# A hybrid decoder block: a reordered opening, whole compression runs, and a diagonal solve in two parts

## The chip, the cores and the metric

The kernel runs on one core of a Trainium2 chip. The metric is the device time of one execution in microseconds (us), and what is compared is the median of several executions. The engines are TensorE (PE in the profile, with its weight loads as PEld), VectorE (DVE), ScalarE (ACT), GpSimd (POOL) and SyncE (SP, which here only issues loads).

## The reference

One layer over 256 tokens of width 1024, float32. Everything below is computed; sizes are those of the run.

```
h = RMSNorm(x)                       # x: 256 x 1024
P = h @ W_in                         # q,k,v,z and a,b of 8 DeltaNet heads; q, 3 x (k,v), gates of NSA
yA = GatedDeltaNet(P_A)              # causal conv of 4 taps, L2 norm, chunked delta rule with a
                                     # unit-triangular solve, gated RMSNorm
yB = NSA(P_B)                        # compressed blocks: silu(blocks @ cmp_w1) @ cmp_w2 for k and v,
                                     # plus selected blocks, plus sliding window
x += (sigmoid(gA) * (yA @ W_pa) + sigmoid(gB) * (yB @ W_pb)) @ W_out
x += (silu(h2 @ W_gate) * (h2 @ W_up)) @ W_down          # h2 = RMSNorm(x)
```

## The kernel before, in words

**Chunks.** The weights come as 87 chunks of 1 MB in the fixed order of the list CHUNKS: gk, gq, gv (four each), kc, vc, then nq mixed with cmpk, then ks, kw, cmpv, vs, vw and gz mixed, the gate and projection chunks mga, pa, mgb, pb, four wo, and at last pairs of gu (w_gate and w_up beside each other) with a dn (w_down) after every pair from the second on. A slot n is what the engines do around chunk n. The kernel writes the order of every engine out by hand; nothing is scheduled at run time.

**Splitting.** A float32 product is made as three products of a rounded high part and a rest: hi by hi, hi by lo, lo by hi. SP loads a chunk into one of three buffers `raw` (a fourth, `raw_ahead`, for nq 0 and nq 2); ACT copies it to `w_hi` (L618), DVE subtracts to `w_lo` (L945), each into one of two buffers, and PE then runs the chunk in two halves (`half_chunk`) of 24 matmuls (L1418 to L1420; in gu L1516 and L1519). Chunk n+1 is split while PE runs chunk n. `load_chunk(n)` waits until the chunk before in the same buffer is split. The chunks cmpk and cmpv (four each) are not split: eight small matmuls (L1493) read `raw` directly, four in each half, with a stage of the delta rule between the halves where slot_stages says so.

**Opening.** SP loads x in one transfer, then ident, then chunk 0 in two halves, and after it has waited for the vectors (vec_in, which ACT queued) chunk 1. PE first runs 32 matmuls on ones (`keep_busy`, L1436), transposes two sets of vectors (L1423), runs 5 more, transposes the normalized x in 16 pieces (`to_channels`), and begins chunk 0. Each engine takes one of the two row blocks of x for the sum of squares (ACT L624, DVE L979); DVE makes rstd from both sums in ten small steps; each engine then scales one block. ACT rounds both halves of chunk 0, then evacuates eight tiles of h (`h_hi`, L635); DVE makes the rest of the first half of chunk 0 (L989) and eight tiles of `h_lo` (L971), POOL makes the second (L525). Chunk 0's first half needs for each row tile k the tiles h_hi and h_lo of that k; its second half repeats all k for the other 128 columns. Between the halves PE makes a bias vector from `relb` and `onehot` (L1761, in ps[6]).

**Diagonal solve.** DVE inverts the 16 x 16 diagonal blocks of the delta rule in `solve_diagonal`, once, in the slot of nq 2 (slot 19) after `split_lo(20)`. POOL then stores the result and loads it back in 16 small transfers, and the stage X4 in slot 24 (cmpv 0) waits for them.

**The feed-forward part.** In the slot after a gu chunk its two sums are evacuated: ACT copies one part (gside, uside), DVE adds the other, multiplies with rstd and frees the banks (usum_done), ACT makes the silu, DVE the product (gu_done), and `evacuate_late` splits the product for dn. In the slots gu 1 and gu 2 this comes after the split of the next chunk, in all others before it. In the slot of gu 0 DVE first makes h_lo of the last two row tiles (`h_low`), then splits gu 1.

Of the kernel before, what the change touches and what calls it, by code (L numbers as in the profile page):

```python
# [145 lines left out]
TAIL = range(AT["gz", 2], AT["pa", 3])  # L146

# [10 lines left out]
def slot_solves(n, half):  # L158
    return (n, half) == (AT["nq", 2], 0)
# [28 lines left out]
def hybrid_block(nc, x, norm1_w, w_in, conv_w, a_log, dt_bias, gdn_norm_w, cmp_pe, cmp_w1, cmp_w2,  # L188
# [5 lines left out]
    with ctx:  # L194
# [124 lines left out]
        stream_ps = ps[0:2]  # L319
        gdn_ps = ps[2:5]  # L320
# [7 lines left out]
        first_hi, first_lo, second_lo = sem("first_hi"), sem("first_lo"), sem("second_lo")  # L328
        raw_first = sem("raw_first")
# [3 lines left out]
        x_in, vec_in, ident_in, const_in, levels_in, small_in, misc_in = sem("x_in"), sem("vec_in"), sem("ident_in"), sem("const_in"), sem("levels_in"), sem("small_in"), sem("misc_in")  # L333
# [136 lines left out]
        def _(sp):  # L470
            sp.dma_start(x_sb[:], x[0].rearrange("(t p) d -> p t d", p=P)).then_inc(x_in, 16)
# [124 lines left out]
        def _(act):  # L596
# [26 lines left out]
            act.wait_ge(x_in, 16)  # L623
            nc.scalar.activation(xn_sb[:, 0, :], x_sb[:, 0, :], ACT.Square, accum_out=scol["x"][:, 0:1]).then_inc(xss, 1)  # L624
            act.wait_ge(rstd_ready, 1)
            nc.scalar.activation(xn_sb[:, 1, :], x_sb[:, 1, :], ACT.Copy, scale=scol["x"][:, 5:6]).then_inc(xn_done, 1)
            act.wait_ge(raw_first, 16)
            nc.scalar.activation(w_hi[0][:, 0:KT // 2, :], raw[0][:, 0:KT // 2, :], ACT.Copy).then_inc(first_hi, 1)
            act.wait_ge(raw_in[0], 16)
# [30 lines left out]
            def evacuate(n):  # L660
                kind, i = CHUNKS[n]
                if kind == "gu":
# [5 lines left out]
                    if i == 0:  # L668
                        act.wait_ge(rows_mm, 1)
                        nc.scalar.activation(rstd_rows[:], ps[6][:, 0:SEQ], ACT.Copy).then_inc(rows_out, 1)  # L670
                    act.wait_ge(gsum_done, i + 1)
# [10 lines left out]
                if kind in ("gk", "gq", "gv"):  # L682
# [3 lines left out]
                    else:  # L686
                        act.wait_ge(pre_dve, 3)
                    nc.scalar.activation(cin[k % 2][:, :, CONV - 1:CONV - 1 + SEQ], bank, ACT.Copy)
                    for a in range(2):
                        ins = nc.scalar.activation(cacc[k % 2][:, a, :], bank[:, a, :], ACT.Copy, scale=tap(k, a, CONV - 1))  # L690
# [167 lines left out]
            for n in range(len(CHUNKS) + 1):  # L858
                kind, i = CHUNKS[n] if n < len(CHUNKS) else (None, 0)
                first_half_out = n < len(CHUNKS) and is_wide(n) and i % 2  # L860
                if n == 0:
                    split_hi(1)
                else:
                    conv_phase = n <= FIRST_STAGE_SLOT
                    if not conv_phase and n not in (AT["gu", 1], AT["gu", 2]):
                        evacuate(n - 1)
# [5 lines left out]
                    if conv_phase or n in (AT["gu", 1], AT["gu", 2]):  # L872
                        evacuate(n - 1)
                    if CHUNKS[n - 1] not in LAST_OF_KIND:
# [55 lines left out]
        def _(dve):  # L930
# [37 lines left out]
            def h_low(before, row, tiles=range(KT)):  # L968
                for k in tiles:
# [8 lines left out]
            dve.wait_ge(x_in, 16)  # L978
            nc.vector.tensor_tensor_reduce(xn_sb[:, 1, :], x_sb[:, 1, :], x_sb[:, 1, :], 1.0, 0.0, ALU.mult, ALU.add,  # L979
                                           accum_out=scol["x"][:, 1:2]).then_inc(xss, 1)  # L980
            dve.wait_ge(xss, TT)
            link(radicand(scol["x"][:, 2:4], scol["x"][:, 0:2], 1.0 / D_MODEL, EPS))
            rsqrt(scol["x"][:, 4:6], scol["x"][:, 2:4], scol["x"][:, 6:8], rstd_ready)
            dve.wait_ge(rstd_ready, 1)
            nc.vector.tensor_scalar(xn_sb[:, 0, :], x_sb[:, 0, :], scol["x"][:, 4:5], None, ALU.mult).then_inc(xn_done, 1)
            dve.wait_ge(pre_pe, 2)
# [6 lines left out]
            link(nc.vector.tensor_copy(cols_a[:], ps[7][:, 0:CONV * 24]))  # L993
            link(nc.vector.tensor_scalar(wk[:], cols_b[:, ROW_KN:ROW_KN + 3], cols_b[:, ROW_QN:ROW_QN + 1], DH ** -0.5, ALU.mult, ALU.mult))
            link(nc.vector.tensor_scalar(zw[:], cols_b[:, ROW_GDN:ROW_GDN + 1], 0.5, None, ALU.mult))
            dve.wait_ge(pre_pe, 3)
            nc.vector.tensor_copy(bias_v[:], ps[6][0:HEADS, 0:384]).then_inc(pre_dve, 1)
# [112 lines left out]
            def solve_diagonal():  # L1110
# [4 lines left out]
                dve.wait_ge(sub_in, 16)  # L1115
                link(nc.vector.memset(sub_t[:], 0.0))
                link(nc.vector.memset(view(sub_t, 0, (down, SUB)), 1.0))
                four = (4 * down, 4)
                link(nc.vector.tensor_copy(view(sub_t, SUB, four), view(sub_m, 1, four)))
                for r in (2, 3):  # L1120
# [3 lines left out]
                for n in (4, 8):  # L1124
# [17 lines left out]
                dve.wait_ge(solved, 1)  # L1142
                nc.vector.tensor_copy(view(sub_tt, 0, (SUB, SUB), (1, SUB)), view(sub_t, 0, (1, SUB), (SUB, SUB))).then_inc(solved, 1)
# [90 lines left out]
            def evacuate(n):  # L1234
                kind, i = CHUNKS[n]
                if kind == "gu":
# [7 lines left out]
                    if i > 0:  # L1244
                        dve.wait_ge(uside, i + 1)
                        nc.vector.tensor_tensor(usum[i % 2][:], usum[i % 2][:], gu_banks(i)[1][:, 0:SEQ], ALU.add).then_inc(usum_done, 1)
                    dve.wait_ge(usum_done, i + 1)
# [59 lines left out]
            for n in range(len(CHUNKS) + 1):  # L1307
                kind, _ = CHUNKS[n] if n < len(CHUNKS) else (None, 0)
                if n == 0:
                    split_lo(1)  # L1310
                else:
                    if n > FIRST_STAGE_SLOT and n not in (AT["gu", 1], AT["gu", 2]):
                        evacuate(n - 1)
# [531 lines left out]
```

## Time and profile before

| what | value |
|---|---|
| median of 3 runs | 580.57 us (580.56 to 581.29) |
| profiled execution, its own time | 580.86 us |
| its span (first to last instruction) | 579.0 us |
| PE busy | 566.9 us, 98% of the span |
| DVE busy | 387.7 us, 67% |
| ACT busy | 299.2 us, 52% |
| POOL busy | 66.5 us, 11% |
| DMA | 98.23 MB, mean 170 GB/s |
| chain that ended last, by engine | PE 88%, DVE 7%, issue 2%, ACT 2% |

PE is busy nearly all the time, so a change can gain in two ways: by taking instructions or their overhead off PE, or by closing the places where PE stands idle before an instruction. In a row of the timeline, the bracket at the end is that idle time with what ended it. "issue" means that nothing in the profile's records explains it.

### The profile page before, as it was taken

The page shows a single profiled execution, that of the slowest core. Times are in us where ns is not written, and L with a number is a line of the kernel's source. Part 1 is how long each engine was busy: PE and PEld are TensorE (multiplying, and loading weights), DVE is VectorE, ACT ScalarE, POOL GpSimd, SP SyncE. Part 2 cuts the span into 40 slices and gives each one's busy share as a digit, 9 for nine tenths or more (in the row PEclk, how much of TensorE's full clock was granted, in tenths as well). Part 3 has the DMA queues.
Part 4 walks back from the last instruction along what each step waited for, and adds up shares of the span by engine and source line. Part 5 has one row for each costly group of instructions (what it writes and reads, how often), then busy time and mean ns, then how long its engine had stood idle before and what let it go on. Part 6 is the DMA issues. An engine that isn't in the chain of part 4 may idle for free.

```text
span 579.0 us, 9820 instructions
## 1 busy us (share of the span) xinstructions
PE 566.9 (98%) x3914; PEld 499.6 (86%) x3914; DVE 387.7 (67%) x624; ACT 299.2 (52%) x470; POOL 66.5 (11%) x81
## 2 busy tenths in 40 slices
PE   9999999999999999989999999999999999999997
PEld 8999999899788888778888888898788888888886
DVE  4778898855766652897865574757756566566664
ACT  5569555515435556637463634366454544545542
POOL 4011210761600000090000000000000000000000
PEclk9999999999999999999999999999999999999999
DMA  7954477595755425423533445575466756667631
GB/s 242 268 180 142 151 192 241 103 294 181 209 148 167 140 79 190 146 77 142 161 132 122 149 168 207 157 198 164 146 192 175 214 180 184 186 179 218 167 124 72
DMA packets 99382, 98.23 MB, mean 170 GB/s; under 512 B 4818, under 2 KB 83719, under 8 KB 99338
## 3 DMA queue, kind: packets, MB, share of 16 engines
q1 hardware_dynamic: 97024, 93.69, 52.6%
q0 software_dynamic: 1808, 2.78, 2.6%
q10 hardware_dynamic: 506, 1.14, 0.6%
q8 instruction: 31, 0.51, 0.4%
q14 instruction: 13, 0.11, 0.1%
HBM read 96.46 MB, written 1.84 MB: 170 GB/s over the span
## 4 chain that ended last, share of the span: by engine, by line
PE 88%; DVE 7%; issue 2%; ACT 2%; POOL 0%; DVEq 0%; ACTq 0%; POOLq 0%
PE ps L1418 18%; PE ps L1420 17%; PE ps L1419 17%; PE ps L1516 13%; PE ps L1519 6%; PE ps L1423 4%; PE ps L1596 4%; DVE w_lo L945 2%; PE ps L1436 2%; PE ps L1751 2%; PE ps L1493 2%; PE ps L1725 1%; PE ps L1627 1%; ACT w_hi L618 1%; DVE cacc L1040 1%
## 5 line engine op out<-in xcount | busy, mean ns | idle before, releaser
L945 DVE TENSOR_TENSOR w_lo<-raw,w_hi 128x2048 fp32r<-128x2048 f32 x76 | 175.2, 2305 | 96.0 <-ACT w_hi L618 95.9
L618 ACT ACTIVATE w_hi<-raw 128x2048 fp32r<-128x2048 f32 x76 | 145.3, 1912 | 81.2 <-PE ps L1420 75.4
L1516 PE MATMUL ps<-h_both,w_hi 128*128 128x512 f32 x352 | 122.8, 397 | 1.0 <-DVE w_lo L945 0.6
L1519 PE MATMUL ps<-h_both,w_lo 128*128 128x256 f32 x352 | 91.1, 279 | 0.0
L1418 PE MATMUL ps<-h_both,w_hi 128*128 128x256 f32 x288 | 82.8, 288 | 0.5 <-DVE h_both L971 0.3
L1419 PE MATMUL ps<-h_both,w_hi 128*128 128x256 f32 x288 | 81.4, 283 | 0.0
L1420 PE MATMUL ps<-h_both,w_lo 128*128 128x256 f32 x288 | 81.4, 283 | 0.0
L1516 PEld LDWEIGHTS ps<-h_both,w_hi 128*128 128x128 f32 x352 | 63.9, 188 | 15.1 <-issue 2.8
L1519 PEld LDWEIGHTS ps<-h_both,w_lo 128*128 128x128 f32 x352 | 66.4, 189 | 3.3
L1418 PE MATMUL ps<-w_hi,h_both 128*128 128x512 f32 (+1 forms) x160 | 58.1, 363 | 4.5 <-DVE zs L1274 2.9
L1418 PEld LDWEIGHTS ps<-h_both,w_hi 128*128 128x128 f32 x288 | 55.1, 191 | 3.8 <-issue 3.6
L1420 PE MATMUL ps<-w_hi,h_both 128*128 128x512 f32 (+1 forms) x160 | 55.6, 348 | 0.0
L1419 PE MATMUL ps<-w_lo,h_both 128*128 128x512 f32 (+1 forms) x160 | 55.5, 347 | 0.0
L1419 PEld LDWEIGHTS ps<-h_both,w_hi 128*128 128x128 f32 x288 | 55.2, 192 | 0.0
L1420 PEld LDWEIGHTS ps<-h_both,w_lo 128*128 128x128 f32 x288 | 55.2, 192 | 0.0
L1418 PEld LDWEIGHTS ps<-w_hi,h_both 128*128 128x128 f32 x160 | 30.2, 189 | 11.6 <-issue 6.0
L1418 PE MATMUL ps<-w_hi,g_hi 128*128 128x512 f32 x88 | 34.4, 391 | 1.1 <-issue 1.1
L1040 DVE SCALAR_TENSOR_TENSOR cacc<-cin,cols_a,cacc 128x256 f32<-128x256 f32 x72 | 35.0, 553 | 0.1
L1420 PE MATMUL ps<-w_hi,g_lo 128*128 128x512 f32 x88 | 34.3, 389 | 0.0
L1419 PE MATMUL ps<-w_lo,g_hi 128*128 128x512 f32 x88 | 34.3, 389 | 0.0
L1420 PEld LDWEIGHTS ps<-w_hi,h_both 128*128 128x128 f32 x160 | 30.2, 189 | 4.0
L1419 PEld LDWEIGHTS ps<-w_lo,h_both 128*128 128x128 f32 x160 | 30.3, 189 | 3.2
(361 smaller groups left out, 938.5 us busy)
## 6 DMA issues: line engine op xcount, KB each, us to landing
raw<-in_w_in SPq DMA_DIRECT2D x31, 1024.0 KB, 5.2
raw<-in_w_gate SPq DMA_DIRECT2D x22, 512.0 KB, 3.9
raw<-in_w_up SPq DMA_DIRECT2D x22, 512.0 KB, 5.2
raw<-in_w_down SPq DMA_DIRECT2D x11, 1024.0 KB, 4.9
raw<-in_cmp_w SPq DMA_DIRECT2D x8, 1024.0 KB, 6.5
raw<-in_w_proj_a SPq DMA_DIRECT2D x4, 1024.0 KB, 5.7
raw<-in_w_proj_b SPq DMA_DIRECT2D x4, 1024.0 KB, 5.1
raw<-in_w_out SPq DMA_DIRECT2D x4, 1024.0 KB, 5.1
```

Of the source, the lines that this page charges most:

```text
L618: nc.scalar.activation(w_hi[s % NSPL][:], raw[RAW_OF[n]][:], ACT.Copy).then_inc(hi_done, 1)
L945: nc.vector.tensor_tensor(w_lo[s % NSPL][:], raw[RAW_OF[n]][:], w_hi[s % NSPL][:].bitcast(f32), ALU.subtract).then_inc(lo_done, 1)
L1040: ins = nc.vector.scalar_tensor_tensor(acc, src[:, a, j:j + SEQ], tap(k, a, j), acc, ALU.mult, ALU.add)
L1418: pe.matmul(bank, lhs(lh), rhs(rh), start=start, stop=False)
L1419: pe.matmul(bank, lhs(lh), rhs(rl), start=False, stop=False)
L1420: return pe.matmul(bank, lhs(ll), rhs(rh), start=False, stop=stop)
L1423: return pe.transpose(o, i, ident[0:n, 0:n])
L1436: pe.matmul(ps[1][:, 0:P], ones_sq[:], ones_sq[:], start=True, stop=True)
L1493: last = pe.matmul(ps[6][g:g + 32, 0:CW], flat[:, i * KT + j, :], raw[RAW_OF[n]][:, j, :], start=(i == 0 and j < 4), stop=(i == 3 and j >= 4))
L1516: cross = lambda stop: pe.matmul(banks[part][:], hi[:, k, part * P:(part + 1) * P], h_both[:, :, k, :], start=(k == 0), stop=stop)
L1519: end = pe.matmul(banks[part][:, 0:SEQ], lo[:, k, part * P:(part + 1) * P], h_hi[:, k, :], start=False, stop=False)
L1596: mm = lambda q, lhsT, rhs, start=True, stop=True: pe.matmul(b4[:, q, :], lhsT, rhs, start=start, stop=stop)
```

## The change

Five things, all on one core and with the same arithmetic:

1. x is loaded in two transfers, one for each row block. DVE sums block 0 and half of block 1, ACT the other half of block 1; one more small DVE step adds the two. Scaling is divided the same way. `keep_busy` runs 20 and 3 times in place of 32 and 5, and the bias matmul moves ahead of the second of them, into ps[1].
2. Chunk 0 runs both column halves for each row tile k (banks ps[0] and ps[6]), hi by hi first, so that only the last pair of each k needs h_lo. ACT rounds the second half of chunk 0 between h_hi tiles 3 and 4. Chunk 1 is split in two halves of rows with semaphores of their own. The copies of conv taps (cols_a) and two small DVE steps move behind that split.
3. The eight compression matmuls of a chunk run in one go, in half 1 for cmpk 0 and in half 0 for all others.
4. `solve_diagonal` runs in two parts: up to blocks of 8 in slot 17 (nq 1, half 1), the rest in slot 19 as before.
5. In the slots gu 2, gu 3 and dn 0 the evacuation is divided: the part that frees the banks ("a") runs before the split of the next chunk, silu and product ("b") after it. In the slot gu 0 `h_low` runs after the split of gu 1.

```diff
+GU_OPENING = (AT["gu", 2], AT["gu", 3], AT["dn", 0])
+def cmp_half(n):
+    return 1 if CHUNKS[n] == ("cmpk", 0) else 0
-def slot_solves(n, half):
-    return (n, half) == (AT["nq", 2], 0)
+SOLVES = {(AT["nq", 1], 1): 0, (AT["nq", 2], 0): 1}
...
-            sp.dma_start(x_sb[:], x[0].rearrange("(t p) d -> p t d", p=P)).then_inc(x_in, 16)
+            for t in range(TT):
+                sp.dma_start(x_sb[:, t, :], x[0, t * P:(t + 1) * P, :]).then_inc(x_tile[t], 16)
... ACT, opening
-            nc.scalar.activation(xn_sb[:, 0, :], x_sb[:, 0, :], ACT.Square, accum_out=scol["x"][:, 0:1]).then_inc(xss, 1)
+            nc.scalar.activation(xn_sb[:, 1, 512:], x_sb[:, 1, 512:], ACT.Square, accum_out=scol["c"][:, 2:3]).then_inc(xss, 1)
...
-            nc.scalar.activation(w_hi[0][:, KT // 2:, :], raw[0][:, KT // 2:, :], ACT.Copy).then_inc(hi_done, 1)
             for k in range(KT):
+                if k == 4:
+                    act.wait_ge(raw_in[0], 16)
+                    nc.scalar.activation(w_hi[0][:, KT // 2:, :], raw[0][:, KT // 2:, :], ACT.Copy).then_inc(hi_done, 1)
... ACT and DVE, slot 0: chunk 1 in two halves
+                    for k, done in ((slice(0, KT // 2), early_hi), (slice(KT // 2, KT), hi_done)):
+                        nc.scalar.activation(w_hi[1][:, k, :], raw[1][:, k, :], ACT.Copy).then_inc(done, 1)
...
             h_low(0, ROW_N1)
+            dve.wait_ge(pre_pe, 3)
+            nc.vector.tensor_copy(bias_v[:], ps[1][0:HEADS, 0:384]).then_inc(pre_dve, 1)
+            for k, split, done in ((slice(0, KT // 2), early_hi, early_lo), (slice(KT // 2, KT), None, lo_done)):
+                nc.vector.tensor_tensor(w_lo[1][:, k, :], raw[1][:, k, :], w_hi[1][:, k, :].bitcast(f32), ALU.subtract).then_inc(done, 1)
+            nc.vector.tensor_copy(cols_a[:], ps[7][:, 0:CONV * 24]).then_inc(cols_set, 1)
... ACT and DVE, every slot n
+                    if not conv_phase and n != AT["gu", 1]:
+                        evacuate(n - 1, "a" if n in GU_OPENING else "ab")
...
+                    elif n in GU_OPENING:
+                        evacuate(n - 1, "b")
... PE, opening
-            keep_busy(32)
+            keep_busy(20)
...
-            keep_busy(5)
-            pe.wait_ge(xn_done, TT)
+            pe.wait_ge(misc_in, 80)
+            pe.matmul(ps[1][0:HEADS, 0:384], relb[:], onehot[:], start=True, stop=True).then_inc(pre_pe, 1)
+            keep_busy(3)
+            pe.wait_ge(xn_done, TT + 1)
... PE, compression chunks
-                    for j in range(half * KT // 2, (half + 1) * KT // 2):
+                    for j in range(KT):
... PE, chunk 0
+                        for k in range(KT):
+                            pe.wait_ge(first_hi if k < KT // 2 else hi_done, 1)
+                            pe.wait_ge(h_hi_done, k + 1)
+                            for o, c in both:
+                                pe.matmul(o, hi[:, k, c], h_hi[:, k, :], start=(k == 0), stop=False)
+                            if k < KT // 2:
+                                pe.wait_ge(first_lo, 1)
+                                for o, c in both:
+                                    pe.matmul(o, lo[:, k, c], h_hi[:, k, :], start=False, stop=False)
+                            pe.wait_ge(h_lo_done, k + 1)
+                            for o, c in both:
+                                pe.matmul(o, hi[:, k, c], h_lo[:, k, :], start=False, stop=False)
+                        pe.wait_ge(second_lo, 1)
+                        for o, c in both:
+                            for k in range(KT // 2, KT):
+                                last = pe.matmul(o, lo[:, k, c], h_hi[:, k, :], start=False, stop=(k == KT - 1))
```

## Rows read from the trace of the kernel before

**Rows 1.** Windows: busy us and instructions by engine, granted clock, DMA share, GB/s.
```profile
229.00:251.00 22.00, 18.91 (x103) 14.84 (x102) 18.82 (x36) 11.28 (x25) 3.72 (x2) 1.00 0.30 100
```

**Rows 2.** Timeline of PE, opening: start us, us, engine, line, what [idle before].
```profile
1.03 9.80 PE L1436 MATMUL ps<-ones_sq 128*128 128x128 f32 x64 [1.03 <-POOL ones_sq L511]
...
11.98 1.91 PE L1423 MATMUL ps<-ident,xn_sb 128*128 128x128 f32 x16
...
14.22 0.36 PE L1418 MATMUL ps<-h_both,w_hi 128*128 128x256 f32 x1 [0.33 <-DVE h_both L971]
...
17.49 0.81 PE L1761 MATMUL ps<-onehot,relb 33*8 33x384 f32 x2
...
21.29 0.36 PE L1418 MATMUL ps<-h_both,w_hi 128*128 128x256 f32 x1
```

**Rows 3.** The same timeline, the other engines of the opening.
```profile
6.04 1.23 DVE L979 CUSTOM_DVE_ANT_0 xn_sb<-x_sb 128x1024 f32<-128x1024 f32 x1 [5.13 <-DMA x_sb<-in_x]
...
9.29 0.75 DVE L985 TENSOR_SCALAR xn_sb<-x_sb,s_x 128x1024 f32<-128x1024 f32 x1
9.59 0.37 SPq L487 DMA_DIRECT2D raw<-in_w_in  x1
...
12.42 2.45 POOL L525 TENSOR_TENSOR w_lo<-raw,w_hi 128x1024 fp32r<-128x1024 f32 x1 [7.12 <-ACT w_hi L630]
...
12.62 3.03 ACT L635 ACTIVATE h_both<-ps,cols_b 128x256 fp32r<-128x256 f32 x8 [0.29 <-PE ps L1423]
13.59 3.23 DVE L971 SCALAR_TENSOR_TENSOR h_both<-ps,cols_b,h_both 128x256 fp32r<-128x256 f32 x8 [0.95 <-ACT h_both L635]
```

**Rows 4.** Timeline of POOL, the last load that the bias matmul waits for.
```profile
3.80 0.54 POOL L521 DMA_DIRECT2D par<-in_dt_bias  x1
```

**Rows 5.** DMA issues: what, queue, count, KB each, us to landing.
```profile
par<-in_dt_bias POOLq DMA_DIRECT2D x1, 4.0 KB, 5.7
```

**Rows 6.** Groups of PE instructions from 3 to 6 us: busy us, mean ns.
```profile
L1436 PE MATMUL ps<-ones_sq 128*128 128x128 f32 x16 | 3.6, 418 | 0.0
```

**Rows 7.** The chain that ended last: start us, us, what (an fp32 matmul counts twice).
```profile
119.20 1.00 PE ps L1493 x16
...
130.08 0.12 PE ps L1418
...
165.54 0.57 PE ps L1493 x8
```

**Rows 8.** Timeline of DVE, slots 19 to 22.
```profile
138.68 2.29 DVE L945 TENSOR_TENSOR w_lo<-raw,w_hi 128x2048 fp32r<-128x2048 f32 x1 [3.46 <-ACT w_hi L618]
140.97 0.27 DVE L1116 MEMSET sub_t<- 128x256 f32 x1
...
144.26 1.08 DVE L1132 TENSOR_TENSOR sub_x<-sub_m,sub_t 128x512 f32<-128x512 f32 x1
...
148.19 2.29 DVE L945 TENSOR_TENSOR w_lo<-raw,w_hi 128x2048 fp32r<-128x2048 f32 x1
```

**Rows 9.** Timeline of PE where chunk 22 (ks) begins.
```profile
150.58 0.36 PE L1418 MATMUL ps<-w_hi,h_both 128*128 128x256 f32 x1 [1.40 <-issue]
```

**Rows 10.** Timeline of PE, starts of gu 1, gu 3 and dn 0.
```profile
395.17 0.47 PE L1516 MATMUL ps<-h_both,w_hi 128*128 128x512 f32 x1 [0.65 <-DVE w_lo L945]
...
407.30 0.48 PE L1516 MATMUL ps<-h_both,w_hi 128*128 128x512 f32 x1 [0.24 <-DVE usum L1246]
...
414.26 0.47 PE L1418 MATMUL ps<-w_hi,g_hi 128*128 128x512 f32 x1 [1.11 <-issue]
```

**Rows 11.** Timeline of DVE, h_low in slot gu 0, split of dn 0.
```profile
391.95 0.88 DVE L971 SCALAR_TENSOR_TENSOR h_both<-ps,cols_b,h_both 128x256 fp32r<-128x256 f32 x2 [2.73 <-ACT h_both L855]
...
411.87 2.29 DVE L945 TENSOR_TENSOR w_lo<-raw,w_hi 128x2048 fp32r<-128x2048 f32 x1 [1.39 <-ACT w_hi L618]
```

**Rows 12.** Timeline of ACT, split of gu 1 and of gu 3.
```profile
388.61 1.92 ACT L618 ACTIVATE w_hi<-raw 128x2048 fp32r<-128x2048 f32 x1 [1.33 <-PE ps L1420]
...
401.74 1.90 ACT L618 ACTIVATE w_hi<-raw 128x2048 fp32r<-128x2048 f32 x1
```

More of the change, by code:

```diff
@@ L670, in evacuate @@
                         nc.scalar.activation(rstd_rows[:], ps[6][:, 0:SEQ], ACT.Copy).then_inc(rows_out, 1)
+                if kind == "gu" and "b" in steps:
                     act.wait_ge(gsum_done, i + 1)
@@ L1123, in solve_diagonal @@
                     link(nc.vector.tensor_reduce(view(sub_t, r * SUB, four, (1, r)), view(sub_x, 0, (r * r, 4), (r, r), (1, r)), AX.X, ALU.add))
-                for n in (4, 8):
+                for n in (4, 8)[part:part + 1]:
                     firsts = range(0, SUB, 2 * n)
@@ L1232, in unit, with evacuate @@
                                             ALU.mult).then_inc(p_done, 1)
-            def evacuate(n):
+            def evacuate(n, steps="ab"):
                 kind, i = CHUNKS[n]
-                if kind == "gu":
+                if kind == "gu" and "a" in steps:
                     dve.wait_ge(gside, i + 1)
@@ L1246, in evacuate @@
                         nc.vector.tensor_tensor(usum[i % 2][:], usum[i % 2][:], gu_banks(i)[1][:, 0:SEQ], ALU.add).then_inc(usum_done, 1)
+                if kind == "gu" and "b" in steps:
                     dve.wait_ge(usum_done, i + 1)
@@ L1308, in _ @@
                 kind, _ = CHUNKS[n] if n < len(CHUNKS) else (None, 0)
[L1309 to L1313, printed above, removed]
+                if n > 0:
+                    if n > FIRST_STAGE_SLOT and n != AT["gu", 1]:
+                        evacuate(n - 1, "a" if n in GU_OPENING else "ab")
                     if CHUNKS[n - 1] in LAST_OF_KIND:
                         evacuate_late(n - 1)
-                    if n == AT["gu", 0]:
-                        h_low(KT, ROW_N2, (KT - 2, KT - 1))
                     if n == AT["ks", 0] + 1:
@@ L1435, in keep_busy @@
                 for _ in range(times):
[L1436 removed]
+                    pe.matmul(ps[0][:, 0:P], ones_sq[:], ones_sq[:], start=True, stop=True)
             pe.wait_ge(ones_set, 2)
[L1439 removed]
+            keep_busy(20)
             pe.wait_ge(ident_in, 16)
@@ L1469, in half_chunk @@
                     hi, lo = w_hi[s % NSPL], w_lo[s % NSPL]
-                    if half == 0 and n > 0:
+                    if half == 0 and n > 1:
                         pe.wait_ge(hi_done, s + 1)
@@ L1473, in half_chunk @@
                         wait_bank(pe, n)
-                elif half == 0:
+                elif half != cmp_half(n):
+                    return None
+                else:
                     pe.wait_ge(raw_in[RAW_OF[n]], 16 * loads_before(n))
@@ L1484, in half_chunk @@
                     c = 0 if kind == "cmpk" else 1
-                    if i == 0 and half == 0:
+                    if i == 0:
                         pe.wait_ge(flat_done, 4 * (c + 1))
@@ new lines, in half_chunk @@
+                    if n == 1 and half == 0:
+                        for k in range(KT):
+                            if k == 0:
+                                pe.wait_ge(pre_dve, 3)
+                                pe.wait_ge(early_hi, 1)
+                                pe.wait_ge(early_lo, 1)
+                            if k == KT // 2:
+                                pe.wait_ge(hi_done, 2)
+                                wait_lo(pe, 1)
+                            last = three(((hi, lo), acts), bank, lambda a: a[:, k, 0:P], lambda a: a[:, k, :], k == 0, k == KT - 1)
+                        return last
@@ L1757, in _ @@
                     last = half_chunk(n, half)
-                    last.then_inc(half_done, 1)
-                    if n == 0 and half == 0:
-                        pe.wait_ge(misc_in, 80)
-                        pe.matmul(ps[6][0:HEADS, 0:384], relb[:], onehot[:], start=True, stop=True).then_inc(pre_pe, 1)
+                    if last is not None:
+                        last.then_inc(half_done, 1)
                     if n == 3 and half == 0:
```

95 lines of the change are left out of this document (55 added, 40 removed).

## The prediction

> **What bounds the kernel now.** I read the shares of busy time first: PE is busy 98% of the span, and 88% of the chain that ended last is PE's. So what counts is PE's own work and the few places where it stands idle. I then read the timeline of PE for idle brackets and went to each that the change touches: before the first matmul on h [rows 2], before chunk 22 [rows 9], and before gu 1, gu 3 and dn 0 [rows 10]. Two further stalls lie between 229 and 251 us, where PE is busy 18.91 of 22.00 us [rows 1]; nothing in the diff touches what they wait for. Last I read the other engines around each place [rows 3, 8, 11, 12] to see what is late next. Everywhere else PE runs without a gap, so a microsecond won at one place reaches the end, as long as the engine that feeds PE there is itself paced by PE.
>
> **Opening.** Before, PE runs 64 matmul records on ones until 10.83 us (1.03 + 9.80), two small transposes, five more calls on ones, and transposes x from 11.98 to 13.89 [rows 2]. But rstd is ready at 9.29 and x is scaled soon after (9.29 + 0.75 on DVE) [rows 3]: PE's own filler makes it late. Now the filler is 24 records shorter. At the pace of the transposes, 1.91 / 16 = 0.12 us each [rows 2], it ends at 10.83 - 24 x 0.12 = 7.95 us. PE then waits for the vectors. SP, which waits for the same ones before it issues chunk 1, issues at 9.59 [rows 3], so they are there just before. The last load for the bias matmul is issued at 3.80 and takes 5.7 us [rows 4, 5], so 9.5: no later. From 9.6 come two small transposes (2 x 0.12), the bias matmul (0.74: its 0.81 less the overlap of two records) and three calls on ones (6 x 0.12): 9.6 + 0.24 + 0.74 + 0.72 = 11.3. Scaled x must be there by then. DVE now sums one and a half blocks: if both halves of x land together at 6.0, that is 1.23 + 0.62, and one step of 0.2 more; rstd comes 0.8 later, at 10.1, and scaling ends at 10.1 + 0.75 + 0.4 = 11.25. If block 0 lands over a microsecond earlier, DVE has it summed by 6.0, and rstd is at about 9.1 and scaling ends at 10.3. Either way 11.3 holds. Transposes of x end at 11.3 + 1.9 = 13.2.
>
> Chunk 0 before takes from 14.22 to 21.29, 7.07 us [rows 2]. Of that 0.74 is the bias matmul. Its 48 matmuls at the steady 0.12 us [rows 7] are 5.76; the other 0.6 is the first half paced by DVE's h_lo, 3.23 / 8 = 0.40 us a tile [rows 3] against 0.36 for three matmuls, and a short gap before chunk 1. With both column halves per tile PE needs 0.72 us a tile in the first four and 0.48 in the last four, both above 0.40. It can also start on hi by h_hi before any h_lo exists. So chunk 0 runs from 13.2 to 19.0, and chunk 1 starts 21.29 - 19.0 = 2.3 us earlier.
>
> What is late next? ACT: h_hi 0 to 3 from 0.64 after the transposes start (as 12.62 is to 11.98), 0.38 a tile, so 11.9 to 13.5; the second half of w_hi, about 1.0, to 14.5; h_hi 4 to 7 to 16.0. PE asks for h_hi 4 at 13.2 + 4 x 0.72 = 16.1. POOL's 2.45 us [rows 3] then ends at 17.0; PE asks for it at 18.0. DVE ends h_lo at 16.9, then the bias copy (some 0.5) and chunk 1's two halves, 1.2 each (half of 2.29 [rows 8] and a little), at 18.6 and 19.8. PE asks at 19.0 and at 19.0 + 12 x 0.12 = 20.4. The margins are 0.4 and 0.6 us, thin but there. Because ACT takes two more small instructions in the evacuation of chunk 0, nothing but DVE's conv 0 waits longer. I take 2.2 us. Lower bound: if the conv slots are paced by DVE and not by PE, only what DVE is ahead counts. Its split of chunk 1 ended at 21.1 before and its three moved small steps now end at 20.4: 0.7 us. Upper bound: the 2.3 us.
>
> The rows also show a state of the clock: from 3 to 6 us a matmul on ones has a mean of 418 ns [rows 6], though the later ones follow each other at 0.12 us, and it was the filler that PE ran in between. Now PE idles from about 7.95 to 9.6. The Trainium skill, "TensorE: Matmul & The Clock Gate", Part 1, says that the throttled state is the default, that activity releases it, and that an idle PE falls back to the lower clock. The trace speaks against it for pauses of this size: with 3.1 us of idle between 229 and 251 the granted clock stays 1.00 [rows 1]. By the row the opening gains 2.2; a fall is a rival below.
>
> **Compression.** Four matmuls in a run take 0.57 us, eight in one run 1.00 [rows 7]: 2 x 0.57 - 1.00 = 0.14 us saved wherever a stage stood between. That is so in cmpk 0 and in the four cmpv. In cmpk 0 the stage now starts 0.57 us earlier, right behind DVE's evacuation of the stage before, so I count nothing there. Four times 0.14 is 0.55 (between 0.4 and 0.7). The stages after a cmpv run get more time for their inputs, and the raw buffer is freed earlier.
>
> **Diagonal solve.** Chunk 22 (ks) waits 1.40 us [rows 9]. Its low part runs on DVE from 148.19 to 150.48, directly behind the solve, which begins at 140.97 [rows 8]. Part 0 is 144.26 - 140.97 = 3.3 us long. In slot 17 it lies in DVE's idle time of 3.46 us before 138.68 [rows 8], just fitting; behind it waits the low part of chunk 20, which PE needs only when it is through with chunk 19. Part 1 then ends 3.3 us earlier, DVE is free at 144.9, and the low part of chunk 22 needs 2.29 after ACT's high part. It suffices that ACT is done by 146.9; DVE found it ready at 148.19. So the whole 1.40 goes. If the high part came late, or part 0 waited for its input from memory, up to 1.4 would stay. The loads that POOL makes from the result also start 3.2 us earlier, so X4 waits for nothing.
>
> **Feed-forward.** In slot gu 0 ACT's high part of gu 1 is done at 390.5 [rows 12], but DVE runs h_low until 392.83 first [rows 11], and gu 1 waits 0.65 [rows 10]. Now the split runs from 390.6 to 392.9, and h_low's first tile ends at 393.3. PE asks for it at about 393.0. So 0.65 goes and about 0.35 comes: 0.3 gained. In the slots gu 2 and gu 3, part "a" ahead of the split frees the banks at once: the 0.24 on usum before gu 3 [rows 10] goes. For dn 0, PE waited 1.11 [rows 10] until the low part ended at 411.87 + 2.29 = 414.16 [rows 11]; DVE itself waited for ACT, which was behind with silu and product of gu 1 and the copies of gu 2. In the new order ACT has in slot gu 3 only two copies (0.7 together) between the end of gu 2 and its high part, and DVE finds it after part "a". I get 409.4 for the high and 411.7 for the low part, on the old scale, against PE's 412.5 on the same scale. The 1.11 goes. In slot gu 2 the copies put ACT's high part of gu 3, at 401.74 before [rows 12], 0.3 later, its low part to 406.3, and PE needs it at 406.7. Together 0.3 + 0.24 + 1.11 = 1.65; if only one of the two thin margins fails, 0.5 less.
>
> **Sum.** 2.2 + 0.55 + 1.40 + 1.65 = 5.8 us. The profiled execution took 580.86 us, which gives 575.1; the median of the runs is 0.29 lower, so 574.8.
>
> **Rivals.** (a) As worked out: 574.8, own range 573.9 to 575.7. Chance 0.62. (b) DVE, not PE, carries the lateness of the opening. For: in the conv slots DVE has 2.29 + 3.2 of every 5.76 us. Against: PE shows no gap there that DVE ends. The opening gives 0.7, in all 4.3: 576.3. Chance 0.14. (c) One of the stalls at ks or dn 0 only changes its cause: 1.1 to 1.4 less, 576.1. For: the fit of 3.3 in 3.46 and two margins under half a microsecond; against: PE needs those parts later than they come. Chance 0.11. (d) The clock falls in the pause after the filler. PE's work from 9.6 on then takes twice as long; for 3 us of it that is 3 us, the opening ends 0.8 later than before, and the total is 2.8 faster: 577.8. By the skill's page this would be the outcome if the pause counted as idle enough; the filler of the kernel before is what speaks for it, the unbroken 1.00 in the row [rows 1] speaks against it. Chance 0.07. (e) Slower: the third load into the first raw buffer waits for POOL's half of chunk 0, which now ends at 17.0 and not 14.87. If the loads then set the pace, each slot takes 1.05 MB at the mean 170 GB/s, 6.2 us in place of 5.76, 0.4 more a slot. It decides from 17 such slots on (7.0 us). Against it: the load is needed at 24.7, 7.7 us after its issue. 582, chance 0.02. (f) The change does not do what it says, because each gain ends in a wait of the next fixed chain, such as those between 229 and 251: 580.5. Against: these chains start from PE. Chance 0.04.
>
> **Range and chances.** From 573.8 to 577.0 hold (a), (b) and (c), some 0.85 with the tails cut. About 0.2%, 1.2 us, is what a measurement can tell from no change. Faster by more: (a) to (d) and a part of (f), 0.95; within it 0.03; slower 0.02.
>
> **What would show it.** Chunk 1's first matmul at 19.1 (late by DVE: a bracket on w_lo before it); the records on ones at 0.12 apart after the pause, else the clock; runs of 1.00 in all eight compression chunks; no bracket before ks; brackets of at most 0.35 in gu 0 and none before gu 3 and dn 0. A new bracket in slots 2 to 12, or a stall that reappears at ks, would make the number wrong.

## The result, and the profile after

The changed kernel takes 575.39 us (median of 4 runs, 574.49 to 576.73) against 580.88 us for the kernel before (4 runs, 580.56 to 581.29). The ratio of the times is 0.991, with a 95% interval of 0.9894 to 0.9923: faster by 5.5 us. The forecast was 574.8 us, in the range 573.8 to 577.0. The profiled execution took 575.23 us, its span is 573.2 us, 5.8 less than before.

The first lines of the page of the changed kernel. PE is still the bound, and busy 4.5 us less; 3.1 of that is filler (46 records on ones in place of 74).

```profile
span 573.2 us, 9771 instructions
## 1 busy us (share of the span) xinstructions
PE 562.4 (98%) x3886; PEld 496.5 (87%) x3886; DVE 390.3 (68%) x629; ACT 298.4 (52%) x472; POOL 66.3 (12%) x81
```

PE's timeline of the opening answers to [rows 2]. Columns as there.

```profile
1.03 7.04 PE L1470 MATMUL ps<-ones_sq 128*128 128x128 f32 x40 [1.03 <-POOL ones_sq L520]
9.71 0.27 PE L1457 MATMUL ps<-ident,rows_a 96*128 96x96 f32 x1 [1.64 <-DMA rows_b<-in_cmp_pe]
...
11.50 1.91 PE L1457 MATMUL ps<-ident,xn_sb 128*128 128x128 f32 x16
13.17 0.48 PE L1596 MATMUL ps<-h_both,w_hi 128*128 128x256 f32 x2
...
19.02 0.28 PE L1452 MATMUL ps<-h_both,w_hi 128*128 128x256 f32 x1
```

Filler until 8.07, a pause of 1.64 us for the vectors, then no gap: chunk 1 starts at 19.02 and not at 21.29. Block 0 of x lands early enough for DVE to start its sum at 4.80, which is the second of the two cases forecast. Behind PE, the engines of [rows 3] finish in time: DVE scaled x by 10.16 (9.68 + 0.48), POOL has the second low part at 17.16, and DVE ends chunk 1's two halves at 19.80. (The lines are from DVE's and POOL's timeline.)

```profile
9.68 0.48 DVE L1010 TENSOR_SCALAR xn_sb<-x_sb,s_x 128x512 f32<-128x512 f32 x1
...
17.46 2.34 DVE L1025 TENSOR_TENSOR w_lo<-raw,w_hi 128x1024 fp32r<-128x1024 f32 x2
```
```profile
14.74 2.42 POOL L534 TENSOR_TENSOR w_lo<-raw,w_hi 128x1024 fp32r<-128x1024 f32 x1 [9.46 <-ACT w_hi L641]
```

The list of PE's waits (total, times, longest) holds all that is left. ("issue" is a wait that nothing in the records explains.) The 1.40 before ks [rows 9] is gone: its first matmul starts at 146.93 with no bracket, 3.65 earlier. The 0.65, 0.24 and 1.11 of [rows 10] are gone too, but 0.54 us stand before gu 3.

```profile
PE ps L1452 <- DVE zs L1308: 3.0, 2, 1.6
PE ps L1457 <- DMA rows_b<-in_cmp_pe: 1.6, 1, 1.6
PE ps L1470 <- POOL ones_sq L520: 1.0, 1, 1.0
PE ps L1457 <- DVE AXb L1102: 0.6, 1, 0.6
PE ps L1556 <- issue: 0.5, 1, 0.5
PE ps L1559 <- DVE h_both L991: 0.3, 1, 0.3
PE ps L1452 <- issue: 0.2, 1, 0.2
```

How far PE is ahead of the kernel before, by the same matmul in both timelines (some of the rows first, those of the changed kernel, then two of the kernel before):

```profile
104.62 0.66 PE L1457 MATMUL ps<-ident,kT 128*128 128x128 f32 x4 [0.58 <-DVE AXb L1102]
...
146.93 0.39 PE L1452 MATMUL ps<-w_hi,h_both 128*128 128x256 f32 x1
...
239.26 0.47 PE L1452 MATMUL ps<-w_hi,h_both 128*128 128x512 f32 x1 [1.40 <-DVE zs L1308]
...
403.07 0.47 PE L1556 MATMUL ps<-h_both,w_hi 128*128 128x512 f32 x1 [0.54 <-issue]
```
```profile
106.95 0.66 PE L1423 MATMUL ps<-ident,kT 128*128 128x128 f32 x4 [0.58 <-DVE AXb L1071]
...
243.45 0.47 PE L1418 MATMUL ps<-w_hi,h_both 128*128 128x512 f32 x1 [1.40 <-DVE zs L1274]
```

| place | before | after | earlier by |
|---|---|---|---|
| chunk 1 | 21.29 | 19.02 | 2.27 |
| the wait on AXb (0.58 in both) | 106.95 | 104.62 | 2.33 |
| first matmul after the stage in cmpk 0 | 115.36 | 113.19 | 2.17 |
| ks | 150.58 | 146.93 | 3.65 |
| first wait on zs (1.40 in both) | 243.45 | 239.26 | 4.19 |
| gu 3 | 407.30 | 403.07 | 4.23 |
| dn 0 | 414.26 | 408.75 | 5.51 |
| last matmul | 575.31 | 569.55 | 5.76 |

### The profile page after: what moved, and what is told of

Same layout as the page of the kernel before. It is cut to its first block, busy times and chain, and to the rows that moved or that the text cites. A ratio compares the mean times of both kernels' runs of the same rounds, so it can differ in the third digit from the quotient of the medians.

```text
span 573.2 us, 9771 instructions
## 1 busy us (share of the span) xinstructions
PE 562.4 (98%) x3886; PEld 496.5 (87%) x3886; DVE 390.3 (68%) x629; ACT 298.4 (52%) x472; POOL 66.3 (12%) x81
## 4 chain that ended last, share of the span: by engine, by line
PE 89%; DVE 6%; ACT 2%; issue 1%; DMA 1%; ACTq 0%; DVEq 0%
PE ps L1452 17%; PE ps L1454 17%; PE ps L1453 17%; PE ps L1556 14%; PE ps L1559 7%; PE ps L1457 4%; PE ps L1660 4%; DVE w_lo L965 2%; PE ps L1815 2%; PE ps L1531 1%; PE ps L1789 1%; DMA rows_b<-in_cmp_pe 1%; PE ps L1691 1%; ACT w_hi L627 1%; DVE cacc L1071 1%
## 5 line engine op out<-in xcount | busy, mean ns | idle before, releaser
L965 DVE TENSOR_TENSOR w_lo<-raw,w_hi 128x2048 fp32r<-128x2048 f32 x75 | 172.9, 2306 | 95.2 <-ACT w_hi L627 95.1
L627 ACT ACTIVATE w_hi<-raw 128x2048 fp32r<-128x2048 f32 x75 | 143.3, 1911 | 78.5 <-PE ps L1454 68.9
L1559 PE MATMUL ps<-h_both,w_lo 128*128 128x256 f32 x352 | 91.3, 280 | 0.3 <-DVE h_both L991 0.3
L1452 PE MATMUL ps<-h_both,w_hi 128*128 128x256 f32 x272 | 77.8, 286 | 0.2 <-issue 0.2
L1453 PE MATMUL ps<-h_both,w_hi 128*128 128x256 f32 x272 | 76.9, 283 | 0.0
L1454 PE MATMUL ps<-h_both,w_lo 128*128 128x256 f32 x272 | 76.9, 283 | 0.0
L1556 PEld LDWEIGHTS ps<-h_both,w_hi 128*128 128x128 f32 x352 | 63.9, 188 | 14.2 <-issue 2.0
L1559 PEld LDWEIGHTS ps<-h_both,w_lo 128*128 128x128 f32 x352 | 66.4, 189 | 4.0 <-issue 0.6
L1452 PEld LDWEIGHTS ps<-h_both,w_hi 128*128 128x128 f32 x272 | 52.1, 192 | 2.5 <-issue 2.5
L1453 PEld LDWEIGHTS ps<-h_both,w_hi 128*128 128x128 f32 x272 | 52.1, 192 | 0.0
L1454 PEld LDWEIGHTS ps<-h_both,w_lo 128*128 128x128 f32 x272 | 52.1, 192 | 0.0
```

Source lines behind the costliest of these rows:

```text
L627: nc.scalar.activation(w_hi[s % NSPL][:], raw[RAW_OF[n]][:], ACT.Copy).then_inc(hi_done, 1)
L965: nc.vector.tensor_tensor(w_lo[s % NSPL][:], raw[RAW_OF[n]][:], w_hi[s % NSPL][:].bitcast(f32), ALU.subtract).then_inc(lo_done, 1)
L1452: pe.matmul(bank, lhs(lh), rhs(rh), start=start, stop=False)
L1453: pe.matmul(bank, lhs(lh), rhs(rl), start=False, stop=False)
L1454: return pe.matmul(bank, lhs(ll), rhs(rh), start=False, stop=stop)
L1556: cross = lambda stop: pe.matmul(banks[part][:], hi[:, k, part * P:(part + 1) * P], h_both[:, :, k, :], start=(k == 0), stop=stop)
```

## The experiments

The kernel before took 580.77 us (18 runs) beside the first four kernels, 580.58 (13 runs) beside the next four, and 580.48 (9 runs) beside the last four.

**The opening alone, and the rest without it.** The first kernel takes from the change only the opening (points 1 and 2); the second only points 3 to 5.

```diff
 open_only: changed kernel, with
-SOLVES = {(AT["nq", 1], 1): 0, (AT["nq", 2], 0): 1}
+SOLVES = {(AT["nq", 2], 0): (0, 1)}
-                    for j in range(KT):
+                    for j in range(half * KT // 2, (half + 1) * KT // 2):
... and evacuation and h_low in the order of before
 rest_only: kernel before, with cmp_half, SOLVES and GU_OPENING of the changed kernel
```

> The opening alone (x in two loads, both halves of chunk 0 per row tile, chunk 1 split in halves, shorter filler); compression, solve and feed-forward as before. If the five parts add up and PE paces the conv slots: chunk 1 begins at 19.0 us as in the changed kernel, and the whole is 2.3 us faster than before (578.6 on a median of 580.9). Rival: the opening's gain reaches the end only together with the others, because DVE or the solve's loads hold their own times; then under 1 us is left, and idle brackets grow at ks or X4.

> Everything but the opening. If the parts add up: 5.6 less 2.3, so 3.3 us faster than before (577.6). If the parts lean on each other (the solve's part 0 fits only because of the opening, or the other way round), it is 2.3 or less, and a bracket stands before ks.

The opening alone: 578.85 us (9 runs, 578.32 to 580.42), 1.9 less; ratio 0.9973 [0.9963, 0.9983]. The rest alone: 577.23 us (4 runs), 3.5 less; 0.9938 [0.9923, 0.9953]. Together 5.46, and the whole change gave 5.49. So the opening's lead is not eaten on the way. In the profile of open_only PE is 3.0 ahead at the AXb wait (this execution's vectors came early, at 8.74), and it keeps that until gu 1. That speaks against DVE pacing the conv slots.

The second kernel showed a wait that the prediction had excluded: the stage X4 on POOL's small loads (PE's timeline).

```profile
165.54 2.08 PE L1646 MATMUL ps<-Db,ATb 64*64 64x64 f32 x64 [0.25 <-DMA DTb<-sub_dt]
```

**The solve alone, the feed-forward part alone.** Kernel before with one point of the change each.

```diff
 solve_only
-    return (n, half) == (AT["nq", 2], 0)
+SOLVES = {(AT["nq", 1], 1): 0, (AT["nq", 2], 0): 1}
 gu_only
+GU_OPENING = (AT["gu", 2], AT["gu", 3], AT["dn", 0])
... evacuate(n - 1, "a" / "b") and h_low as in the change
```

> The diagonal solve in two parts alone. Theory: the bracket of 1.40 us before ks goes and nothing else changes, 1.4 us faster (579.5). Rival: part 0 in slot 17 is held up by GpSimd's clearing of Db, as the 1.49 us copy of the changed kernel suggests, so far that chunk 20 is late; then a new bracket before nq 3 and less than 1 us gained.

> The feed-forward opening alone (evacuation in two parts, h_low behind the split of gu 1). Theory from the trace of the changed kernel: gu 1 0.3 us earlier, gu 3 no earlier than that less its new wait of about 0.5, dn 0 about 1.3 earlier, and 0.2 to 0.3 more behind it: 1.5 us faster (579.4). Rival: the wait before dn 0 went only because the kernel was 4 us ahead of its loads; then it stands here again, and under 0.5 us is gained.

Solve: 579.36 us (10 runs), 1.4 less, 0.9977 [0.9968, 0.9987], and no bracket before ks. Feed-forward: 578.48 us (4 runs), 2.3 less, 0.9961 [0.9946, 0.9975]. The last matmul of the second is 2.41 earlier, but 0.35 of that is there already in the opening, which this kernel doesn't change (first matmul on h at 13.86, not 14.22: the 64 filler records end at 10.18 here and at 10.83 there). That leaves 2.1, more than in the whole change (1.57). rest_only, which also has the old opening, gains 2.0 there. Part of the difference stands before gu 3: a wait of 0.19 in both, 0.54 in the changed kernel.

**The pause of PE in the opening.** The first filler is cut to 2 calls, so that PE idles 6.9 us.

```diff
-            keep_busy(20)
+            keep_busy(2)
```

> The changed kernel with 2 calls on ones in place of the first 20, so PE stands idle from about 2 us until the vectors land (8.7 to 9.7 us in the traces so far). Theory of the clock: the pause is now long, PE comes out of it at the lower of its two levels, the 16 transposes of x take over 3 us and the first matmuls on h follow each other at 0.21 to 0.24 us; chunk 1 begins 2 to 3 us later and the whole is 2 to 3 us slower than the changed kernel. Rival: the filler is of no use, chunk 1 begins at the same time, no difference.

```profile
9.13 0.39 PE L1457 MATMUL ps<-ident,rows_a 96*128 96x96 f32 x1 [6.88 <-DMA rows_b<-in_cmp_pe]
...
12.41 3.43 PE L1457 MATMUL ps<-ident,xn_sb 128*128 128x128 f32 x16
```

578.25 us (10 runs, 576.84 to 580.55), 0.9961 [0.9945, 0.9976], 2.9 more than the changed kernel. The transposes of x take 3.43 us in place of 1.91, chunk 0 runs at full pace from 15.6, and chunk 1 starts at 21.43: 2.41 later, though the vectors came 0.58 earlier, so 3.0 us by the clock. The ten runs lie in two groups of five, 576.84 to 577.65 and 578.84 to 580.55; the profile is of the first (577.61, 2.4 more than the profiled execution of the changed kernel), and what the second group lost on top is not known.

**The compression chunk of the delta stage.** cmpk 0 runs its matmuls in half 0, ahead of the stage between the halves.

```diff
 def cmp_half(n):
-    return 1 if CHUNKS[n] == ("cmpk", 0) else 0
+    return 0
```

> The changed kernel with the whole compression run of cmpk 0 in half 0, ahead of the stage that transposes, and not behind it. Theory: the changed kernel lost 0.16 us there because the 16 transposes start right behind the stage before, wait for its banks and stretch from 2.00 to 2.29 us; with the run of 1.00 us ahead they take 2.00 again and the saving of 0.14 comes: 0.3 us faster than the changed kernel, seen in the trace rather than in the median. Rival: the stretch is due to ACT's copies of the transposes, which then wait still: no difference.

Between the AXb wait and the first matmul behind the stage lie 8.18 us (106.71 to 114.89), against 8.57 in the changed kernel (104.62 to 113.19) and 8.41 before. So this order gains 0.39 there, and keeps it: the zs wait comes 134.24 us after the AXb wait, 134.64 in the changed kernel. Yet the time is 576.72 us (4 runs, 576.45 to 577.01), 0.9929 [0.9914, 0.9944]: 1.3 more than the changed kernel. The opening shows why (PE's timeline, then windows with PEclk, the granted clock, third from the end):

```profile
10.18 0.27 PE L1457 MATMUL ps<-ident,rows_a 96*128 96x96 f32 x1 [2.37 <-DMA rows_b<-in_cmp_pe]
...
11.97 3.40 PE L1457 MATMUL ps<-ident,xn_sb 128*128 128x128 f32 x16
...
21.11 0.28 PE L1452 MATMUL ps<-h_both,w_hi 128*128 128x256 f32 x1
```
```profile
12.00:15.00 3.00, 3.00 (x18) 3.00 (x16) 1.19 (x4) 2.14 (x5) 0.00 (x0) 0.53 1.09 365
15.00:18.00 3.00, 3.00 (x25) 3.00 (x24) 2.22 (x7) 3.00 (x7) 2.42 (x1) 0.90 1.11 337
```

This is what rival (d) describes: the vectors landed late, the pause was 2.37 us, and then, with PE busy again, the clock fell to half for about 3 us. Chunk 1 is 2.09 late: 0.47 by the vectors, 1.38 by the transposes (3.05 us from the first of them to the first matmul on h, in place of 1.67) and 0.25 by the first matmuls on h. So the low clock cost 1.6 us. The edit lies at 112 us, and nothing of it runs in the opening; that all four runs of this kernel had the low clock (0.997) stays unexplained.

**The memset of Db, and gu 0's silu and product.** In the changed kernel DVE's small copy at the head of part 0 takes 1.49 us; before, the same copy took 0.17. POOL's memset runs at the same time.

```profile
133.50 1.49 DVE L1151 COPY sub_t<-sub_m 128x4 f32<-128x4 f32 x1
```
```profile
133.16 1.80 POOL L579 MEMSET Db<- 128x2048 f32 x1 [5.16 <-DVE w_lo L965]
```

One kernel puts the memset behind the stores of the solve, the other gives silu and product of gu 0 to the slot of gu 2.

```diff
 db_late
-            nc.gpsimd.memset(Db[:], 0.0).then_inc(d_init, 1)
             pool.wait_ge(solved, 1)
...
             pool.dma_start(sub_dt, sub_tt[:]).then_inc(sub_back, 16)
+            nc.gpsimd.memset(Db[:], 0.0).then_inc(d_init, 1)
 gu0_late, ACT and DVE
+                    if n == AT["gu", 2]:
+                        evacuate(n - 2, "b")
+                        evacuate_late(n - 2)
-                        evacuate(n - 1)
+                        evacuate(n - 1, "a" if n == AT["gu", 1] else "ab")
```

> The changed kernel with GpSimd's clearing of Db moved from before the solve's result to behind the two stores of it. Theory: the 4-element copy that takes 1.49 us in part 0 of the solve takes so long only because GpSimd clears Db (1.80 us) at the same time; it takes 0.17 again, the low part of chunk 20 starts at about 136.5 instead of 137.6, the result is there 1.1 us earlier, and PE is not faster since it did not wait: no difference in time (within 0.1 us). Rival: the copy waits for its input from memory; then it stays 1.5 us long or gets a bracket.

> The changed kernel with silu, product and high part of gu 0 moved from slot gu 1 to slot gu 2, behind the split of gu 3. Theory: gu 3 waits 0.54 us (0.19 in two other runs) because ACT's split of gu 3 stands behind silu, product and g_hi of gu 0, which wait on rstd and DVE; with them moved the split starts about 1.2 us earlier and the bracket before gu 3 goes: 0.2 to 0.5 us faster. Rival: the wait only moves on to dn 0, whose high and low parts of gu 0 and gu 1 now come later: no gain, a bracket before dn 0.

```profile
133.23 0.17 DVE L1151 COPY sub_t<-sub_m 128x4 f32<-128x4 f32 x1
```

The copy is back at 0.17 and the next split starts 1.1 us earlier behind it; but PE needs 134.63 us from the AXb wait to the zs wait (104.36 to 238.99), against 134.64. The median, 574.83 us (4 runs, 0.9894 [0.9878, 0.9911]), is the changed kernel's. The stretched copy was real and hidden. With gu0_late, 574.77 us (4 runs, 0.9895 [0.988, 0.991]), the bracket before gu 3 is gone, but the wait has moved one chunk on, to dn 0 (PE's timeline):

```profile
408.04 0.47 PE L1458 MATMUL ps<-w_hi,g_hi 128*128 128x512 f32 x1 [0.38 <-issue]
```

**Closing the pause; x in one load; all together.** A repeat of the changed kernel stands beside them.

```diff
 filler_26
-            keep_busy(20)
+            keep_busy(26)
 x_one_load
-            for t in range(TT):
-                sp.dma_start(x_sb[:, t, :], x[0, t * P:(t + 1) * P, :]).then_inc(x_tile[t], 16)
+            sp.dma_start(x_sb[:], x[0].rearrange("(t p) d -> p t d", p=P)).then_inc(x_tile[0], 16)
 best_26: filler_26 with the edits of cmpk0_first, db_late and gu0_late
```

> The changed kernel once more, beside the kernel with the longer filler. Theory (the clock falls in the pause in some executions): most runs at 574.4 to 575.6, some one in four at 576.3 to 577.2 with a mean granted clock of 0.997 or less. Rival (one execution was disturbed by something else): all within 574.3 to 575.8.

> As the changed kernel, but the first filler is 26 calls in place of 20, so that PE idles about 0 to 0.7 us instead of 1.2 to 2.4 us before the vectors come. Theory (the pause lets the clock fall in some executions, and then costs 1.6 to 2 us): no execution shows the fall, transposes of x at 0.12 us each in the profile, the median is 574.5 to 575.0 and all runs lie within 0.6 us of each other. Rival (the spread comes from when the vectors land and not from the clock): median and spread as those of the repeat of the changed kernel, or 0.2 to 0.7 higher, because the longer filler ends behind the vectors in the executions where they land early.

> As the changed kernel, but x comes in one transfer; the division of the sums and of the scaling stays. In the changed kernel DVE had the scale at 9.7 us and PE began the transposes of x only at 11.5, behind the vectors, the bias matmul and the filler. Theory (the two transfers bring nothing): DVE's sum of block 0 begins 1 to 1.5 us later, scaled x is ready at 10.3 to 11.2, the time is as the repeat of the changed kernel within 0.3 us. Rival (DVE's chain is then late, since it sums one and a half blocks): a bracket on the scaled x before its transposes and 0.3 to 1 us more.

> The changed kernel with four edits: cmpk 0 runs in half 0 like the others, the memset of Db comes behind the stores of the solve, silu and product of gu 0 move one slot later, and the first filler is 26 calls. Theory: cmpk 0 gives 0.4, the two others 0.1 to 0.2 each, and the clock never falls: median 573.9 to 574.4, so 0.6 to 1.0 below the changed kernel's. Rival (the gains of the last two are noise and cmpk 0's ends in the next fixed chain): within 0.3 of the kernel that has only the longer filler.

| kernel | median us (runs) | single runs | ratio |
|---|---|---|---|
| changed, again | 575.02 (4) | 574.56, 574.83, 575.22, 576.47 | 0.9908 [0.9895, 0.9922] |
| filler_26 | 575.54 (4) | 574.95, 575.42, 575.66, 575.98 | 0.9912 [0.9899, 0.9926] |
| x_one_load | 575.78 (4) | 575.12, 575.34, 576.22, 576.49 | 0.9917 [0.9904, 0.9931] |
| best_26 | 574.50 (5) | 574.11, 574.16, 574.50, 574.65, 576.18 | 0.9899 [0.9886, 0.9913] |

*The clock.* Of the 8 runs of the changed kernel two have a mean granted clock of 0.997, and they are the 576.73 and the 576.47; the other six are 574.49 to 575.56. With the filler of 20 calls such a clock (0.997 or less) came in 10 of 33 runs, over all kernels with the new opening (4 of the 10 are those of cmpk0_first); with 26 calls in 1 of 9 (the 576.18). That points the way the theory says, but the counts are too small to show that the longer filler cures it. In the profiled executions pauses of 0.17 to 1.64 us went without a fall; those of 2.07 (x_one_load) and 2.37 us were followed by one.

*x.* With one transfer DVE's sum of block 0 starts at 6.01, not 4.80, and scaled x is ready at 11.34 (the prediction had 11.25 for this case). The vectors came at 9.32, and the transposes came 1.07 us after the last filler began, in place of 0.77: 0.3 us of waiting for x. So the second transfer would have been worth 0.3 here, where the vectors were early; with vectors later by that much it would be worth nothing (an argument, not a run). Medians can't tell 575.78 from 575.02, because two of the four runs had the low clock.

*The longer filler didn't pay* in its profiled execution, and the loss is not in the opening. Up to the AXb wait filler_26 is 0.26 ahead of the changed kernel (104.36); at the zs wait it is 0.88 behind (240.14). The stage X4 lies between (timelines of PE, ACT and SP of filler_26):

```profile
164.97 0.68 PE L1691 MATMUL ps<-Db,ATb 64*64 64x64 f32 x16 [0.73 <-ACT AXb L791]
```
```profile
161.38 1.91 ACT L627 ACTIVATE w_hi<-raw 128x2048 fp32r<-128x2048 f32 x1 [5.74 <-DMA raw<-in_w_in]
```
```profile
147.29 1.56 SPq L496 DMA_DIRECT2D raw<-in_w_in  x1
```

and the same two instructions of the changed kernel:

```profile
159.79 1.91 ACT L627 ACTIVATE w_hi<-raw 128x2048 fp32r<-128x2048 f32 x1 [3.93 <-DMA raw<-in_w_in]
```
```profile
147.52 0.53 SPq L496 DMA_DIRECT2D raw<-in_w_in  x1
```

This weight load was under way for 12.3 us in the changed kernel, 14.1 in filler_26 and 13.6 in best_26; before, ACT never waited for it (issued at 150.56, split at 159.42). ACT splits it when it lands, and only then evacuates the tiles that X4 needs. In the changed kernel that split ends at 161.70, 1.2 us before X4 begins; in filler_26 it ends at 163.29, 0.7 us after X4 has begun. In filler_26 X4 with its surroundings takes 6.19 us (162.63 to 168.82) and in best_26 5.68, against 5.08 in the changed kernel. So in the profile of best_26 the 0.39 of cmpk 0 (seen again: 104.13 to 112.31 is 8.18) is lost at X4, and what is left, 0.5 us by medians, is within the intervals. No kernel of these is shown to be faster than the changed one.

The loss does not come from being earlier. In filler_26 the load is issued as long after the AXb wait as in the changed kernel (42.93 us, 42.90); gu0_late, at 104.18 even further ahead, lost nothing (134.64 us to the zs wait); cmpk0_first issued it 0.39 sooner, as best_26 did, had it in 12.2 us and kept its gain. What sets the two profiles apart is SP's issue, 1.56 and 1.36 us long; in the seven other profiles with the whole change it is 0.53 or 0.54, and the load takes 11.6 to 12.5. In both, a load of instructions (queue q8 in the list of DMA queues) falls between 146 and 147 us, beside that issue; in the changed kernel it comes between 152 and 153. A longer filler means more instructions for PE, which could move that load, but that this stretches the issue is not shown, and with one profile of each kernel the two may also be chance.

## Why the prediction was right, step by step

**Opening, 2.2: measured 2.27 at chunk 1 and 2.33 at 106 us.** The times on the way were forecast as 7.95, 9.6, 11.3, 13.2 and 19.0, and came as 8.07, 9.71, 11.50, 13.17 and 19.02. Both h parts were in time and POOL too. "9.5: no later" for the last load of the bias matmul held only because the vectors were late: in open_only, where they came at 8.74, the bias matmul waited another 0.22 us for that load. The single row that the rest hangs on, the time when the vectors land, is the one that varies: 8.74 to 10.18 us in the eight profiles where PE waited for them. My sum took one execution's value for a constant.

**Compression, 0.55: measured 0.38.** Between ks and the zs wait, where the four cmpv lie, 0.54 are gained (3.65 to 4.19): as forecast. In cmpk 0 I had counted nothing; it loses 0.16 (2.33 to 2.17), since with the stage first the transposes of AXb (109.97) come while ACT is still splitting a chunk (until 110.58), and wait for ACT to evacuate them: 16 take 2.29 us in place of 2.00. cmpk0_first shows that the other order would gain.

**Solve, 1.40: measured 1.4 in solve_only,** and 3.65 - 2.17 = 1.48 in the change. Part 0 took 4.6 us and not 3.3, because of the copy; the low part of chunk 20 started 1.1 us later against PE than before, and PE still didn't wait for it. The margin was larger than the 3.46 I compared it with, since what counts is when PE asks. "X4 waits for nothing" was wrong as a rule: it waited 0.25 in rest_only for exactly these loads.

**Feed-forward, 1.65: measured 1.57** (5.76 - 4.19), by two errors that cancel. The step that failed is gu 3: "its low part to 406.3, and PE needs it at 406.7". On that scale, which is the time here plus 4.23, the low part ended at 407.2 (402.97 + 4.23), and 0.54 was waited. The low part was late because ACT's high part was, at 402.89 in place of the forecast 402.0: its two copies cost 0.53 and not 0.3, and the silu of gu 0 in front of them came 0.62 later than before (401.06, 400.44), which the sum had left out. Against it, 0.25 us come after dn 0 has begun, which I hadn't seen: before, dn 0 to gu 4 took 5.78 us, and all later dn chunks 5.45, because DVE ended the split of gu 4 at 419.93 and PE began it at 420.04. The backlog of dn 0 had reached one chunk further, without a bracket. gu 0's new wait on h_low was 0.33, forecast 0.35.

Part of the 0.54 belongs to the opening, some 380 us earlier, and how stays open. With point 5 and the old opening (gu_only, rest_only) DVE starts the split of gu 2 0.1 us after ACT has it, and the bracket before gu 3 is 0.19; with the new opening it is 0.46 us after, in each profile, and the bracket 0.54 to 0.57 (none in gu0_late and best_26, where the order differs). open_only shows the same 0.35 over the kernel before (0.81 against 0.46), here as a wait with no cause in the records:

```profile
394.34 2.29 DVE L965 TENSOR_TENSOR w_lo<-raw,w_hi 128x2048 fp32r<-128x2048 f32 x1 [0.27 <-issue]
```

That it hangs on where DVE's instructions lie in its stream is a guess that no run tested.

**Sum.** 2.33 - 0.16 + 0.54 + 1.48 + 1.57 = 5.76 at the last matmul, against 5.8 forecast. By the medians it is 5.49, and the forecast time of 574.8 is 0.6 below the measured one.

**The rivals.** (b) is refuted by the table: the 2.3 of chunk 1 are there at 106 us, behind all conv slots. (c) didn't come at ks or dn 0; a stall of that kind, 0.54, came at gu 3, where one of the thin margins failed. (e) wasn't seen in the opening; its mechanism, a load that lands late, was found at X4. (f) is refuted by the two equal waits between 229 and 251 us, each reached 4.2 us earlier. (d) I had at 0.07 and 3 us for a whole result; it is a matter of single executions, two of eight of this kernel, and costs about 1.6 us by the runs. I had doubled 3 us of work, so lost 3 us; by the two windows of cmpk0_first (granted 0.53 and 0.90) some 3.4 us pass at half rate (3 x 0.47 / 0.5 + 3 x 0.10 / 0.5), in which 1.7 us of work are done and 1.7 are lost. The row I set against it, the unbroken 1.00 between 229 and 251 us [rows 1], was the wrong witness: there PE's idle time comes in several pieces, the longest 1.6 us. The rule of the Trainium skill ("TensorE: Matmul & The Clock Gate", Part 1) that an idle PE falls back to the lower clock agrees with the 0.53 above. The median escaped because in six of eight runs the clock stayed up; the row that my chance of 0.07 rested on was no ground for that, so it was luck.

## What to carry to other kernels

When PE is the bound, price each edit by the matmul behind it and read the lead at a handful of fixed places; that sum held to 0.1 us here, though two errors in it cancelled. A filler that is cut to fit a transfer should be set against the transfer's latest landing, not the one in the profile: its end and the landing both vary (though here the longer filler was not shown to pay). And when several stalls are removed, look again at the loads behind them: one weight load that nothing waited for before is now split only 1.2 us ahead of the stage behind it, and in the two executions in which it took longer PE waited.

## What the runs showed of the hardware

- The granted clock fell after the pause, not in it: in cmpk0_first PE was busy again for 1.8 us (10.18 to 11.97) at full pace before the slow transposes. In filler_short, where PE had run only four records on ones before its pause, the windows show 1.00 from 9 to 15 us while 16 transposes take 3.43 us, so the column can't be trusted ahead of the first fall; the spacing of the records can.
- A DVE copy of 128x4 elements took 1.49 us beside a GpSimd memset and 0.17 without. It ended at 134.99, the memset at 134.96 (the ends of GpSimd's instructions are rough), while two DVE memsets in the same time kept their 0.27 and 0.07. The trace agrees with the Trainium skill, "SBUF — State Buffer", "Who interferes with whom": a DVE copy can use the port pair it shares with GpSimd, and whoever comes second is blocked until the other's whole instruction is done. I had not applied it when I put 3.3 us on part 0.
- A 1 MB weight load took 11.6 to 14.1 us from issue to use in the kernels with the whole change, and at most 8.9 in the kernel before. With part of the change it is in between: 9.4 with the solve alone, 10.1 with all but the opening, 10.4 with the opening alone. POOL's 16 small loads overlap it in both, and the DMA share is as high (1.12 from 153 to 159 us, and 1.13 from 156 to 162 before), so which of the transfers ahead of it holds it up stays open.
